# First tile's loads by need, half the weight stores one tile later, eight PSUM banks in one pool, the second exp as a square on GpSimd, v with 512 columns

## What is computed

```python
z = rmsnorm(x) @ w_in                       # -> xa, ga, u, v, gates (6 x 1024 columns)
xc, _ = causal_conv(xa, prev, conv_w, conv_b)          # branch A
r = sigmoid(xc @ w_a + b_a);  i = sigmoid(xc @ w_x + b_x)   # block-diagonal
log_a = -8 * r * softplus(-lam)
a = exp(log_a);  mult = sqrt(1 - a^2)
h = scan(a, mult * (i * xc))                # h_t = a_t h_{t-1} + ...
o_a = (h * gelu(ga)) @ w_br_a
vn = layernorm(gelu(v))                     # branch B
o_b = (gelu(u) * (masked w_s @ vn + b_s)) @ w_br_b
mix = (sigmoid(g_a) * o_a + sigmoid(g_b) * o_b) @ w_out
x = x + rmsnorm(mix)
gate, up = split(rmsnorm(x) @ w_ffn_in)
x = x + rmsnorm((silu(gate) * up) @ w_ffn_out)
```

## Time and profile before

| | |
|---|---|
| Median of 3 runs (lowest to highest) | 2374.91 us (2367.84 to 2399.89) |
| Profiled execution: its own time, its span | 2359.24 us, 2357.7 us |
| Spans of the eight cores | 2340.2 to 2357.7 us |
| Busy: PE, PEld, DVE, ACT, POOL | 2083.0, 1036.2, 1109.8, 950.9, 401.0 us |
| Matmuls with 512 columns, hnT and fring | 629.9 us for 2750 |
| ACT table loads | 101, 129.6 us |
| Software queue (POOL's loads), hardware queue (SP's) | 10.8%, 56.5% of 16 engines' span |

### The profile page before, as it was taken

One profiled execution on the slowest core, in us unless ns is written; L12 is line 12 of the kernel. 1 busy time (PEld: TensorE's weight loads), 2 busy tenths in 40 slices (PEclk: granted clock), 3 DMA queues, 4 the chain that ended last, 5 costly groups with the idle time before them and its releaser, 6 DMA issues.

```text
span 2357.7 us, 40038 instructions; the slowest of 8 cores (2340.2 to 2357.7 us)
## 1 busy us (share of the span) xinstructions
PE 2083.0 (88%) x12022; PEld 1036.2 (44%) x12231; DVE 1109.8 (47%) x1613; ACT 950.9 (40%) x1530; POOL 401.0 (17%) x743
## 2 busy tenths in 40 slices
PE   1568899987799988999899988999899999999796
PEld 1334355442454444444444444444444445444342
DVE  1474367321574257623664147633665247622331
ACT  2572276211573146512563147512563136512210
POOL 2233233120110121011200121101210111001000
PEclk9789999998899999999999999999899999999898
DMA  9879789899554676555855676556755666555556
GB/s 219 208 170 185 173 216 230 208 250 289 175 162 148 186 246 200 146 158 179 285 162 148 180 234 216 144 155 185 264 179 148 176 222 216 146 156 159 184 152 204
DMA packets 233377, 451.68 MB, mean 192 GB/s; under 512 B 27088, under 2 KB 27152, under 8 KB 233168
## 3 DMA queue, kind: packets, MB, share of 16 engines
q1 hardware_dynamic: 212784, 412.07, 56.5%
q0 software_dynamic: 20384, 37.04, 10.8%
HBM read 432.49 MB, written 53.54 MB: 206 GB/s over the span
## 4 chain that ended last, share of the span: by engine, by line
PE 74%; DMA 8%; issue 6%; ACT 6%; DVE 4%; POOL 1%; SPq 1%; ACTq 0%; DVEq 0%; POOLq 0%; another core or an unknown queue 0%
PE ps L531 73%; DMA xpre<-xp 3%; DMA xres<-xp 2%; ACT junk L537 1%; DVE xres L711 1%; DVE XC L776 1%; ACT EE L537 1%; DMA fring<-wsc 1%; DMA yp<-xres 1%; PE ps L684 1%; ACT L537 1%; DVE tokf L702 1%; DMA mring<-wt 1%; POOL stats L598 1%; ACT xsb L537 1%
## 5 line engine op out<-in xcount | busy, mean ns | idle before, releaser
L531 PE MATMUL ps<-xnT,mring 128*128 128x512 bf16 x2496 | 603.3, 386 | 51.7 <-ACT gga L537 41.7
L531 PE MATMUL ps<-hnT,fring 128*128 128x512 bf16 x2750 | 629.9, 380 | 5.1 <-DVE hnT L687 1.5
L531 PEld LDWEIGHTS ps<-hnT,fring 128*128 128x128 bf16 x2816 | 274.1, 98 | 327.3 <-issue 5.6
L537 ACT ACTIVATE T<-ps 128x512 f32<-128x512 f32 x259 | 153.9, 598 | 645.2 <-PE ps L531 606.7
L531 PEld LDWEIGHTS ps<-xnT,mring 128*128 128x128 bf16 x2560 | 247.7, 99 | 339.8 <-issue 70.3
L531 PE MATMUL ps<-fring,ffT 128*128 128x512 bf16 x1370 | 349.8, 394 | 39.0 <-ACT junk L537 32.4
L997 DVE SCALAR_TENSOR_TENSOR T<-T,ps 128x512 f32<-128x512 f32 x130 | 89.4, 688 | 386.6 <-PE ps L531 386.6
L531 PEld LDWEIGHTS ps<-fring,ffT 128*128 128x128 bf16 x1408 | 139.3, 101 | 206.7 <-issue 62.3
L1138 DVE SCALAR_TENSOR_TENSOR sgt<-sgt,ps 128x512 f32<-128x512 f32 (+2 forms) x182 | 122.3, 675 | 212.5 <-ACT sgt L537 211.9
L537 ACT ACTIVATE sgt<-ps 128x512 f32<-128x512 f32 (+2 forms) x182 | 106.9, 592 | 239.9 <-PE ps L531 206.2
L1014 POOL TENSOR_TENSOR VM<-T 128x512 bf16<-128x512 f32 x64 | 81.0, 1266 | 617.1 <-DVE T L997 499.4
(11 more groups left out here) (115 smaller groups left out, 1904.1 us busy)
## 6 DMA issues: line engine op xcount, KB each, us to landing
fring<-wsc SPq DMA_DIRECT2D x660, 256.0 KB, 3.0
mring<-wsc SPq DMA_DIRECT2D x568, 256.0 KB, 3.2
mring<-wt POOLq DMA_DIRECT2D x72, 256.0 KB, 8.7
wsc<-mring SPq DMA_DIRECT2D x72, 256.0 KB, 8.1
fring<-wt POOLq DMA_DIRECT2D x66, 256.0 KB, 7.3
wsc<-fring SPq DMA_DIRECT2D x66, 256.0 KB, 6.6
xpre<-xp SPq DMA_DIRECT2D x32, 512.0 KB, 6.3
xres<-xp SPq DMA_DIRECT2D x32, 512.0 KB, 5.8
```

Source lines behind the costliest of these rows:

```text
L531: P.op("pe", lambda e: e.matmul(out, lhsT=lhsT, rhs=rhs, start=start, stop=stop), reads=reads, writes=writes, cost=max(27.0, n / 2.4 + 2.5))
L537: P.op("act", lambda e: e.activation(out=out, in_=in_, func=func, **kw), reads=reads, writes=writes, cost=165.0 + 0.833 * n + 93.0 * aps + ...
```

## The change

It does seven things.

1. **Loads by need.** Tile 0's four x sub-tiles go straight into the residual slots and are loaded first; `s_loadx` is called from `s_pn`, for tiles from 1 on. The constants are split in three: what the gates need at once; `row_loads` and `row_sums` after the third and seventh xa unit; `late_loads` after the third merge gate unit. `after=P.mark()` makes such a transfer wait for the last matmul recorded so far; the fring loads (`fr.after`) wait for a matmul in the merge part.
2. **Stores.** `STORE_AT` gives the use at which a piece is stored. W_XA, W_GA, W_U, W_GTA, W_FG and W_FU (76 of the 138) are read as float32 in their first and second tile and stored in the second.
3. **Banks.** Mixer and feed-forward part draw on one pool `a`. The samples have `s` until their last bank is bound; then its four banks join `a`.
4. **Square.** `s_exp`: the second Exp is gone, GpSimd computes EE = AA * AA; the first Exp is no longer in the atomic block, the two Sqrt are.
5. **v.** The host lays the v weights out so that a piece holds two k-rows of 512 columns: 8 matmuls of 512 columns in place of 32 of 128.
6. **Feed-forward part.** FFN_SPAN is 0.92. The last four weight pieces of an output half (NLAST) are taken sub-tile by sub-tile. The samples' output product rides with the first half, so the third reading of W_FO goes. The stages of both parts are now recorded merged in the order of their keys.
7. **Last sub-tile.** The last tile's fourth sub-tile has its residual in xpre, whose use is over by then.

```diff
-FFN_SPAN = 0.96
+FFN_SPAN = 0.92
-POOLS = dict(m=(0, 1, 2, 3), f=(4, 5, 6, 7))
+POOLS = dict(a=(0, 1, 2, 3), s=(4, 5, 6, 7))
+def STORE_AT(pid):
+    if pid < W_V or W_GTA <= pid < W_GTB or W_FG <= pid < W_FO:
+        return 1
+    return 0
...
-                    avail[vb["pool"]].append((max(x.end for x in vb["nodes"]), vb["phys"], v))
-                    avail[vb["pool"]].sort()
+                    p = "s" if vb["pool"] == "s" and first["s"] < len(order["s"]) else "a"
+                    avail[p].append((max(x.end for x in vb["nodes"]), vb["phys"], v))
+                    if p == "a" and first["s"] == len(order["s"]):
+                        avail[p] += avail["s"]
+                        avail["s"] = []
+                    avail[p].sort()
...
-                    if pid not in seen:
-                        seen.add(pid)
+                    u = uses.get(pid, 0)
+                    uses[pid] = u + 1
+                    at = STORE_AT(pid)
+                    if u <= at:
                         P.op("pool", lambda e: e.dma_start(out=buf[:, s, :], in_=wt[pid, :, :]), writes=[cell],
-                             dma_sem=self.pls[s], serial=True, cost=950.0, nbytes=1 << 19)
-                        P.op("sp", lambda e: e.dma_start(out=wsc[pid, :, :], in_=buf[:, s, :]), reads=[cell],
-                             writes=[("wsc", pid)], dma_sem=self.sts[s], serial=True, cost=70.0, nbytes=1 << 18)
+                             dma_sem=self.pls[s], serial=True, cost=950.0, nbytes=1 << 19, after=self.after)
                     else:
                         P.op("sp", lambda e: e.dma_start(out=buf[:, s, :], in_=wsc[pid, :, :]), reads=[("wsc", pid)],
                              writes=[cell], dma_sem=self.ls[s], serial=True, cost=70.0, nbytes=1 << 18)
+                    if u == at:
+                        P.op("sp", lambda e: e.dma_start(out=wsc[pid, :, :], in_=buf[:, s, :]), reads=[cell],
+                             writes=[("wsc", pid)], dma_sem=self.sts[s], serial=True, cost=70.0, nbytes=1 << 18)
...
+            def late_loads():
+                cdma(lambda e: e.dma_start(out=gbc_pm[:], in_=g_post_mix.partition_broadcast(128)), writes=[("gbc_pm",)], nbytes=1 << 19, after=P.mark())
+                cdma(lambda e: e.dma_start(out=gbc_pf[:], in_=g_post_ffn.partition_broadcast(128)), writes=[("gbc_pf",)], nbytes=1 << 19, after=P.mark())
+                fr.after = P.mark()
...
+            def xbuf(i, s):
+                if i == NT - 1 and s == NSUB - 1:
+                    return xpre[:, 0, :], ("xpre", 0), xp_sems[0], y_sems[NSUB + 1]
+                x = (4 * i + s) % (NSUB + 1)
+                return xres[:, x, :], ("xr", x), xr_sems[x], y_sems[x]
...
-                            for q in range(4):
-                                for k in range(NCH):
-                                    mm(128, ps[0:PT, b, q * 128:(q + 1) * 128], lhs_of(k), got[q][0][:, k, :], k == 0, k == NCH - 1,
-                                       [vc[q]] + reads, [("ps", b)])
+                            for k in range(NCH):
+                                mm(512, ps[0:PT, b, :], lhs_of(k), got[k // 2][1][:, (k % 2) * 512:(k % 2 + 1) * 512], k == 0, k == NCH - 1,
+                                   [vc[k // 2]] + reads, [("ps", b)])
...
                 def s_exp(cs):
+                    for c in cs:
+                        sl = c % NS
+                        act(512, AA[:, sl, :], EE[:, sl, :], AF.Exp, [("EE", sl), ("hcn",)], [("AA", sl)], table="exp", aps=2,
+                            scale=hcn[:, c:c + 1], bias=hcn[:, c:c + 1])
+                        pool(1150.0, lambda e, sl=sl: e.tensor_tensor(out=EE[:, sl, :], in0=AA[:, sl, :], in1=AA[:, sl, :], op=ALU.mult),
+                             [("AA", sl)], [("EE", sl)])
                     with P.atomic("act"):
-                        for c in cs:
-                            sl = c % NS
-                            act(512, AA[:, sl, :], EE[:, sl, :], AF.Exp, [("EE", sl), ("hcn",)], [("AA", sl)], table="exp", aps=2,
-                                scale=hcn[:, c:c + 1], bias=hcn[:, c:c + 1])
-                            act(512, EE[:, sl, :], EE[:, sl, :], AF.Exp, [("EE", sl), ("cneg",)], [("EE", sl)], table="exp", aps=2,
-                                scale=cneg[:, c:c + 1], bias=cneg[:, c:c + 1])
...
-                    with P.atomic("pe"):
-                        for ss in range(2):
-                            s = 2 * p + ss
-                            for h in range(2):
-                                b = S["fo"][2 * ss + h]
-                                mm(512, ps[:, b, :], ffT[:, j, s * 128:(s + 1) * 128], w[:, h * 512:(h + 1) * 512], j == 0, j == NFF - 1,
-                                   [cell, ("ffT", j)], [("ps", b)])
+                    got = [fr.get(W_FO + jj) for jj in range(j, j + (NLAST if j == NFF - NLAST else 1))]
+                    for ss in range(2) if len(got) > 1 else (None,):
+                        with P.atomic("pe"):
+                            for jj, (_, w, cell) in enumerate(got, j):
+                                for sx in (ss,) if ss is not None else range(2):
+                                    s = 2 * p + sx
+                                    for h in range(2):
+                                        b = S["fo"][2 * sx + h]
+                                        mm(512, ps[:, b, :], ffT[:, jj, s * 128:(s + 1) * 128], w[:, h * 512:(h + 1) * 512], jj == 0, jj == NFF - 1,
+                                           [cell, ("ffT", jj)], [("ps", b)])
...
-                    for j in range(NFF):
-                        add(0.43, lambda j=j: s_sfout(j))
```

192 lines of the change are left out of this document (112 added, 80 removed).

## The result

The changed kernel takes **2229.9 us** (median of 4 runs, 2227.4 to 2232.3) against 2368 to 2400 for the kernel before on the same chip. The ratio is 0.940, 95% interval 0.937 to 0.944: 6.0% faster. I had forecast 2268; the time lies in the range, 38 us under the forecast.

A forecast was written before the change was run, and what follows sets the result against it. The prediction saw transfers and first-tile latencies as the bound up to 592 us, then TensorE with a few repeating waits, then a tail. Terms -34 - 6 - 42 - 25 = -107 took 2374.9 to 2268 us, range 2200 to 2335.

The forecast's parts named there:

- First two tiles: Start to the end of tile 1: earlier x loads and 20 us less transfer work end it at 558, -34 us.
- Third tile: Tile after the first two: takes on more float32 readings and stores, yet gains 6 us (0 to 12).
- Steady tiles: Five later tiles: waits, lost clock and v gain, ScalarE costs; net -8.4 us each, -42 in all.
- the two waits: TensorE in a steady tile, waiting for gga and for junk: both go with the pool of eight banks, -11 us.
- I charge 6 us to the path: ScalarE in the scan part: ten more table loads, less eight Exp, cost each steady tile 6 us.
- v: The v matmuls of a steady tile: 512 columns instead of 128 save 1.4 us.
- The end: From the last out-projection matmul, 166 us before: x load wait and gap between output halves go, -25 us (-18 to -30).
- The squares: GpSimd, 8 x 1.27 us a tile: its time is free, the latency is within the 6 us charged.
- Rival 3: All of it pays, in every part of the kernel: -168 us, 2207 us; chance 0.12.
- Rival 1: ScalarE and GpSimd eat the steady gain, so steady tiles stay at 266 us: 2310 us; chance 0.13.
- rival 4: Slower: Exp, square, Sqrt become serial in every pair, squares held by VectorE: 2453 us, 3.3% slower; chance 0.04.
- rival 2: Transfers do not fall, so tiles 0 to 2 stay at 860 us: 2308 us; chance 0.12.

The follow-up runs named there:

- Run 8: Changed kernel with only the FG and FU pieces stored at their second use, all others at their first; 2229.1 us undisturbed, ratio 0.937.
- run 9: Changed kernel with every piece stored at its first use, as in the kernel before; 2218.4 and 2226.5 us undisturbed, ratio 0.936.
- run 10: Changed kernel with the first tile's x sub-tiles again going through the two xpre buffers and loaded a second time for the residual; 2241.1 us, ratio 0.944.
- run 7: Changed kernel with late transfers (row constants, broadcasts, first eight feed-forward pieces) no longer waiting for any matmul; 2229.9 us, ratio 0.938.
- run 4: Changed kernel with v again as 32 matmuls of 128 columns a unit; 2233.8 and 2234.9 us undisturbed, ratio 0.938.
- run 5: Changed kernel with two exponentials on ScalarE again and no GpSimd square, the Exp loose, only the two Sqrt in a block; 2229.6 us, ratio 0.938.
- run 2: Changed kernel with the old block of four Exp and two Sqrt on ScalarE and no GpSimd square; 2255.8 us, ratio 0.948.
- run 6: Changed kernel with banks split four and four from the third tile, the old Exp and Sqrt block, and NLAST = 1; 2307.0 us, ratio 0.971.
- run 1: Changed kernel with banks split four for the mixer and four for the feed-forward part from the third tile on; 2266.0 us, ratio 0.952.
- run 3: Changed kernel with banks split four and four from the third tile and the old Exp and Sqrt block; 2275.5 us, ratio 0.955.
- run 11: Kernel before with two edits alone, NLAST = 4 and the two exponentials loose on ScalarE; 2393.0 us, ratio 1.008.

## Why the prediction was right, and where it was not

**First two tiles.** I forecast that tile 1 would end at 558, and it ends at 559. That is luck. I took 592 us for its end before; it was 612, so the forecast of -34 stands against a measured -53. And the working did not hold. I expected tile 0 near 250 (it is 267) and tile 1 near 308 (292), and I had derived the gain from 20 us less transfer work. Run 8 has 31 us less of that work than the changed kernel and run 9 34 us more than run 8, and tile 1 ends at 555 and 563 us. What the runs show: x in front, about 10 us (run 10); holding transfers back, nothing (run 7).

For the second tile (tile 1), 25 us shorter, the trace of the kernel before shows what I had priced as transfer time alone (-17). At its end the samples' output product reads the 22 FO pieces a third time, from 565.84 to 588 us, and TensorE waits nine times for a piece, 8.6 us in all. Then it stands 11.34 us, in the row at 604.00 above. The samples hold a residual slot until their own y is stored, and the norm of this tile's first sub-tile needs that slot:

```profile
592.03 0.48 SPq L1190 DMA_DIRECT2D ys<-xres  x1
594.97 0.34 SPq L1027 DMA_DIRECT2D xres<-xp  x1
598.56 1.28 DVE L711 SCALAR_TENSOR_TENSOR xres<-tokm,stats,xres 128x1024 f32<-128x1024 f32 x1 [6.60 <-DMA xres<-xp]
```

All eight cores have this wait, 11.3 to 13.1 us. TensorE's idle time in the second tile fell from 38 to 17 us, and these two places are 20 us. That the third reading's end freed both is read from the rows; no run puts it back. The rest (the merged order, eight banks from tile 1 on) was not taken apart.

**Third tile**, forecast -6 (0 to -12), measured +18 by the same cut. Its transfers do bind (run 9 takes them out and gets 255), and more than I took; DMA is 0.90, not the 0.83 I named. Part of the rest is the kernel before: at 612 us it had no feed-forward matmul of the first tile left, and its third tile has TensorE busy for 238 us against 248 now. The three tiles together were forecast at -40 and measured at -35, so the wrong cut did not move the sum by much.

**Steady tiles**, forecast -8.4 each with bounds of -14 and 0, measured **-15.6**, outside the bounds. This is the step that failed: 36 us more than forecast, of which the early tiles and the end give 11 back, so that the sum is -132 and not -107. (The other 13 of the 38 us are the 15.7 that I kept between profiled execution and median; it is 2.2 now.) Term by term: idle time fell by 10.2 us a tile, forecast 11 for the two waits. Busy time fell by 5.4, of which v is 1.3 (run 4); the other 4.1 I put down to the granted clock, 1.00 instead of 0.98, for which I had 2. And 6 us were charged for ScalarE that cost nothing. So the size of the waits was right, and two things were wrong in what I took for their causes and in what I charged against them:
- "I charge 6 us to the path" for ten more table loads a tile. They are there (180 loads in all, forecast 179) and cost nothing: run 5 has another 24 and takes the same time. The loose Exp, which I priced by its loads alone, gained 5.4 to 5.6 us a tile, and between runs 2 and 5 the block is all that differs, so it is the order that gains. That ScalarE was busy 16.5 of 20 us in a stretch was true and not a bound, since other matmuls stood ready with banks to write to.
- I booked both waits, 11 us, to the bank pool. The one for junk goes by NLAST even with split banks, and I had counted NLAST in the end only (run 6: 5.0 us a tile). The one for gga goes with the pool or, mostly, with the loose Exp.

By runs, a tile: 266.4 before, 262.8 (run 6: recording, span, x loads, v), 257.8 with NLAST, 250.8 with banks and loose Exp together. The first 3.6 us were not taken apart, but for v's 1.3 us of busy time.

**v**, -1.4 a tile: the busy time fell so, the tile did not (run 4).

**The end**, forecast -25, measured -19. The 15 us wait is now 5.1 us, where I had it gone; the pool gave 8 to 10 (run 1).

**The squares.** No wait on them is seen. Half of the 64 squares take 1.03 or 1.04 us; the mean is 1.26. Some are held by VectorE, as I had read from the copies, and the longest lies across four convolution instructions:

```profile
1906.05 2.73 DVE L824 SCALAR_TENSOR_TENSOR XC<-xa,cpk,XC 128x512 f32<-128x512 f32 x4
1906.42 3.26 POOL L908 TENSOR_TENSOR EE<-AA 128x512 f32<-128x512 f32 x1 [2.42 <-ACT AA L557]
```

The price on the other side I had not named: the convolution's instruction takes 793 ns in the mean, and 748 in run 5, which has no squares. Within the changed kernel the 33 of 192 that overlap a square take 1030 ns and the others 744. The Trainium skill (SBUF — State Buffer, SBUF: two separate sides) says that of such a pair the instruction that starts first keeps the shared ports to its end and the other is blocked. The rows agree in kind.

**The rivals.** Rival 3, all of it pays (0.12), priced the steady tiles at -14 and the first three at -68; the first was nearly right and the second, measured at -35, was not. Rival 1 falls by steady tiles of 250.8 us, rival 4 by the time itself and by squares that no one is seen to wait for; rival 2 falls by the result and is right in one thing, that fewer transfers alone move little.

## What to carry to other kernels

Where an order is planned, price a part's freedom and not only its work: an atomic block that saves table loads can cost more than they do, and one more load is free while the engine in front has other work with a place to put it. Two waits that end on the same engine may have different causes (a bank pool, a chain at a half's end), so undo one part at a time before booking both to one. And a gain of a few microseconds at a seam depends on the whole order: the same two edits gained 7 us a tile in one program and nothing in the other, because there, among other things, a residual slot came free too late. Last, check a cut in a trace against the same instruction of every sub-tile: here one wrong boundary would have shown -33 and -2 us where a gain of 53 and a loss of 18 stood.

## What the runs showed of the hardware

A table load followed by its ACTIVATE costs its own 1283 ns and no more: one at 1100.76 us is followed by a GELU at 1102.06. The Trainium skill (ScalarE: Activation LUTs, What ACT_TABLE_LOAD costs) adds a drain of 1.38 us to each; over the 180 loads that would be an estimated 248 us, and the rows show none of it. After each of the 180 loads the next instruction of ScalarE starts within 13 ns of the load's end, and half of the loads start within 18 ns of the instruction ahead of them:

```profile
1100.76 1.28 ACT L557 ACT_TABLE_LOAD   x1
...
1102.06 0.60 ACT L557 ACTIVATE gga<-ps 128x512 f32<-128x512 f32 x1
```

Over the five steady tiles TensorE's granted clock is lower where its idle time is longer: 1.00 with 13 to 23 us of idle (the changed kernel, runs 4 and 5), 0.99 with 35 to 41 us (runs 1 to 3), 0.98 with 60 and 74 us (run 6 and the kernel before), 0.97 with 85 us (run 11). No run moves the one without the other. In the changed kernel the busy time of a tile fell beside the idle time, by 5.4 us, of which v explains 1.3.
